# Zeroed products ahead of the input, the first weights in a tile of their own, and one input tile on another queue, in a two-layer DeltaNet and attention kernel

## The chip, the core and the metric

The kernel runs on one core of a Trainium2 chip. The metric is the device time of one execution in microseconds (us), lower is better; the text gives the median of the runs. TensorE (PE in the profile, with its weight loads as PEld) multiplies, VectorE (DVE), ScalarE (ACT) and GpSimd (POOL) do the elementwise work, and SyncE (SP) issues transfers. ScalarE issues transfers too, on a queue of its own. All engines run their own instruction lists and meet only at semaphores.

## The reference

The program computes two layers on an input `x` of 1024 tokens by 1024 channels, in float32. Layer 0 is a gated DeltaNet: one projection, a short causal convolution with SiLU on q, k and v, the delta rule in chunks, a gated RMS norm and an output projection. Layer 1 is sliding-window attention with sinks and rotary positions.

```python
def reference(x, a_w_in, a_conv, a_a_log, ..., ln_g, ln_b):
    for i in range(DEPTH):                      # DEPTH = 2
        if kind == 0:
            y = _gated_deltanet(x, a_w_in[j], a_conv[j], a_a_log[j], a_dt_bias[j], a_norm_g[j], a_w_out[j])
        elif kind == 1:
            y = _swa_sinks(x, b_w_in[j], b_sinks[j], b_w_out[j], pos)
        ...
        x = _layernorm(DEEPNORM_ALPHA * x + y, ln_g[i], ln_b[i])

def _gated_deltanet(x, w_in, conv_w, a_log, dt_bias, norm_g, w_out):
    qkv, z, beta_logit, a_logit = jnp.split(x @ w_in, ...)     # w_in: 1024 x 4112
    qkv = _causal_conv_silu(qkv, conv_w)
    ...                                                        # the delta rule in chunks
    o = _rmsnorm(_unchunk(o), norm_g).reshape(bsz, t_len, GDN_V)
    o = o * jax.nn.silu(z.astype(f32))
    return o.astype(x.dtype) @ w_out
```

## The kernel before, in words

Every projection keeps float32 accuracy by splitting both factors into a high and a low part and adding three products: high by high, high by low, low by high. TensorE wants the channels of `x` on the partitions, and the input comes with tokens there, so the kernel begins by turning it.

**The start.** SP issues eight transfers of 512 KB, one for each tile `t` of 128 tokens, into `tok` (L492), and then four small ones: the convolution's rows (L493), two bias rows and the norm's gains (L494 to L496). ScalarE issues the 16 gate columns of the weight matrix into the front of `w_raw` (`fetch(-1)`, L1151). GpSimd makes the identity, a triangle and zeroed stretches (L594 to L605), each of which counts up `s_const`.

`turn_input(t)` (L715 to L724) waits for tile `t` and turns it in two halves, `n = 2t` and `n = 2t + 1`, each of four 128x128 transposes into one of four PSUM banks. For each half ScalarE rounds the bank to `act_hi` (L1177), then VectorE subtracts to get `act_lo` (L1476), and a bank is free for half `n` once VectorE is done with half `n - 4` (`s_xlo`). TensorE's list is: tiles 0 to 4, then the first half of the gates' product on 512 tokens (`project_input_gates(0, 0)`, L688, which waits for the first eight `act_lo`), tile 5, the second half of that product, tile 6, six products of the first projection tile (`project(0, ...)`, L708), tile 7, the turned convolution rows (L740), and the rest of the projection.

**The weights.** A projection tile `w` is 1024 x 128. ScalarE fetches it into `w_raw` (`fetch(w)`, L1154), rounds it to `w_hi` (`high(w)`, L1160), and VectorE subtracts to get `w_lo` (`low(w)`, L1463). There is one `w_raw`, and the gate columns sit in it too, so `fetch(0)` waits for VectorE's part of the gate columns (L1469) and is issued ahead of half 4 (`FETCH_AT`). `high(0)` stands ahead of half 10 (`HIGH_AT`) on ScalarE, `low(0)` ahead of half 10 on VectorE.

**What follows.** 64 groups of 24 products each (32 weight tiles by two halves of 512 tokens) are laid out for TensorE, ScalarE and VectorE by a table of places (`plan`), with the delta rule of eight heads put between them. For each head VectorE makes `nT`, SP carries its diagonal blocks out and in, GpSimd inverts them in 31 steps (L643, L646), SP carries them back (L527), VectorE sets them out (L1660 to L1663), and TensorE's `level(h, 0)` (L839) waits for that. Layer 0's output stage, layer 1's projections and attention, and its output stage follow.

Only the two buffers `k_dec[1]` and `state` of the later work matter here: `k_dec[1]` is first written for head 1, `state` after the first chunk of head 0.

Of the kernel before, what the change touches and what calls it, by code (L numbers as in the profile page):

```python
# [21 lines left out]
F32 = mybir.dt.float32  # L22
# [4 lines left out]
P = 128  # L27
# [159 lines left out]
def hybrid_trunk(nc, x, a_w_in, a_conv, a_a_log, a_dt_bias, a_norm_g, a_w_out, b_w_in, b_sinks, b_w_out,  # L187
# [9 lines left out]
    with ctx:  # L197
        def sem(name):
            return ctx.enter_context(nc.semaphore(name))
# [154 lines left out]

        s_const = sem("s_const")
        s_x = [sem(f"s_x{t}") for t in range(NT)]
        s_small = sem("s_small")
        s_crow = sem("s_crow")
        s_gates = sem("s_gates")
        s_xtr = sem("s_xtr")  # L360
# [2 lines left out]
        s_ctr = sem("s_ctr")  # L363
        s_cw = sem("s_cw")
        s_wraw = sem("s_wraw")
        s_whi = sem("s_whi")
        s_wlo = sem("s_wlo")
        s_group = sem("s_group")
# [108 lines left out]
        def bank_free(eng, g):  # L477
# [3 lines left out]
            else:  # L481
                eng.wait_ge(s_zt, g - QKV_GROUPS + 1)

        def channel_tile(w):

            return (w % 3) * GH + w // 3 if w < QKV_TILES else w
# [2 lines left out]
        @block.sync  # L489
        def _(sp):  # L490
            for t in range(NT):
                sp.dma_start(tok[:, t, :], x[0, t * P:(t + 1) * P, :]).then_inc(s_x[t], 16)  # L492
            sp.dma_start(conv_rows, a_conv[0].rearrange("k (w p) -> (k w) p", p=P)).then_inc(s_crow, 16)  # L493
            sp.dma_start(bias2[:, 0, :], a_dt_bias[0].partition_broadcast(P)).then_inc(s_small, 16)  # L494
            sp.dma_start(bias2[:, 1, :], a_a_log[0].partition_broadcast(P)).then_inc(s_small, 16)
            sp.dma_start(norm_g[:, :], a_norm_g[0].rearrange("(p a) -> p a", a=1)).then_inc(s_small, 16)  # L496

            sp.wait_ge(s_gr, 2)
            sp.dma_start(gc_rows.rearrange("r (c j) -> (r c) j", c=4), o_tok[0:64, 0, :]).then_inc(s_gio, 16)
# [6 lines left out]
            for h in range(GH):  # L506

                sp.wait_ge(s_m, NT * (h + 1))
                for b in range(4):
                    sp.dma_start(blocks_in[h % 2].rearrange("(c b) j i -> b j c i", b=4)[b],  # L510
                                 nT[h % 2][32 * b:32 * b + 32, :, 32 * b:32 * b + 32]).then_inc(s_pin, 16)
                sp.wait_ge(s_pin, 64 * (h + 1))
                for g in range(4):
                    sp.dma_start(blocks[32 * g:32 * g + 32, :, :], blocks_in[h % 2]).then_inc(s_pb, 16)

                if h + 1 < GH:
                    gc_broadcast(h + 1)
                sp.wait_ge(s_inv, h + 1)
                for g in range(4):
                    sp.dma_start(blocks_out[h % 2][:, g:32:4, :], inverse[32 * g:32 * g + 32, :, :]).then_inc(s_pout, 16)  # L520
                sp.wait_ge(s_pout, 64 * (h + 1))
                if h >= 2:
                    sp.wait_ge(s_y, NT * (h - 1))
                elif h == 0:
                    sp.wait_ge(s_const, 14)
                for b in range(4):
                    sp.dma_start(xT[h % 2][32 * b:32 * b + 32, :, 32 * b:32 * b + 32],  # L527
                                 blocks_out[h % 2].rearrange("(c b) j i -> b j c i", b=4)[b]).then_inc(s_xt, 16)
# [62 lines left out]
        @block.gpsimd  # L591
        def _(pool):
            steps = Link(pool, s_const)
            steps.next(pool.memset(ident[:, :], 0.0))  # L594
            steps.next(pool.memset(tri, 1.0))
            steps.next(pool.memset(w_raw[:, :, 16:P], 0.0))
# [82 lines left out]

        @block.tensor  # L680
        def _(pe):
            pe.wait_ge(s_const, 6)

            def project_input_gates(b, k0):

# [49 lines left out]
            project(0, 0)  # L735
            project(0, STEP)
            turn_input(NT // 2 + 3)
            pe.wait_ge(s_crow, 16)
            rows = CONV_K * QKV_TILES
            pe.transpose(ps[:, 2, 0:rows], conv_rows, ident[0:rows, 0:rows]).then_inc(s_ctr, 1)  # L740
            for q in range(2 * STEP, GROUP, STEP):
# [401 lines left out]
        def _(act):  # L1143
            own = Link(act, s_act)

            def fetch(w):

                if w >= 0:
                    act.wait_ge(s_wlo, w + 1)
                if w < 0:  # L1150
                    act.dma_start(w_raw[:, :, 0:16], wa_tiles[:, :, GATE_COL:GDN_IN]).then_inc(s_wraw, 16)  # L1151
                else:
                    c0 = P * channel_tile(w)
                    act.dma_start(w_raw[:, :, :], wa_tiles[:, :, c0:c0 + P]).then_inc(s_wraw, 16)  # L1154

            def high(w):
                act.wait_ge(s_wraw, 16 * (w + 2))
                if w >= 1:
                    act.wait_ge(*((s_gates, 2) if w == 1 else (s_group, 2 * w - 2)))
                act.activation(w_hi[w % 2][:, :, :], w_raw[:, :, :], ACT.Copy).then_inc(s_whi, 1)  # L1160

            fetch(-1)
            act.wait_ge(s_const, 4)
            act.activation(w_hi[1][:, :, 32:P], w_raw[:, :, 32:P], ACT.Copy)
            for n in range(2 * NT):
                if n == 2:
                    act.wait_ge(s_wraw, 16)
                    act.activation(w_hi[1][:, :, 0:16], w_raw[:, :, 0:16], ACT.Copy).then_inc(s_whi, 1)
                if n == FETCH_AT:
                    fetch(0)  # L1170
                if n == HIGH_AT:
                    high(0)
# [285 lines left out]
        def _(dve):  # L1458
            own = Link(dve, s_dve)

            def low(w):
                dve.wait_ge(s_whi, w + 2)
                dve.tensor_tensor(w_lo[w % 2][:, :, :], w_raw[:, :, :], w_hi[w % 2][:, :, :].bitcast(F32),  # L1463
                                  ALU.subtract).then_inc(s_wlo, 1)

            for n in range(2 * NT):
# [4 lines left out]
                if n == HIGH_AT:  # L1471
# [7 lines left out]
            dve.wait_ge(s_ctr, 1)  # L1479
            dve.tensor_scalar(convw[:, :, :], ps[:, 2, 0:CONV_K * QKV_TILES].rearrange("p (k w) -> p k w", k=CONV_K),  # L1480
                              0.5, None, ALU.mult).then_inc(s_cw, 1)
            dve.wait_ge(s_small, 48)
            own.next(dve.tensor_scalar(norm_g[:, :], norm_g[:, :], 0.5, None, ALU.mult))
            def piece(g, k):

# [449 lines left out]
```

## Time and profile before

| | |
|---|---|
| median of 3 runs | 1054.86 us |
| lowest and highest | 1054.53 and 1057.03 us |
| the profiled execution: its own time | 1057.3 us |
| the profiled execution: its span | 1055.6 us |
| TensorE busy | 1027.4 us, 97% of the span |
| VectorE, ScalarE, GpSimd busy | 679.0, 498.6, 250.0 us |
| TensorE's granted clock, mean | 0.99 of full speed |

Times in the trace count from the first recorded instruction. A row of a timeline is a run of like instructions: start, how long they took together, the engine, the line, and in brackets how long the engine was idle before them and what released it. The releaser is inferred: a wait on several semaphores is put down to the one that came last by the profile, and where the engine named had long been done, it was another. The page's own row for the clock is in tenths of full speed.

### The profile page before, as it was taken

The page shows a single profiled execution, that of the slowest core. Times are in us where ns is not written, and L with a number is a line of the kernel's source. Part 1 is how long each engine was busy: PE and PEld are TensorE (multiplying, and loading weights), DVE is VectorE, ACT ScalarE, POOL GpSimd, SP SyncE. Part 2 cuts the span into 40 slices and gives each one's busy share as a digit, 9 for nine tenths or more (in the row PEclk, how much of TensorE's full clock was granted, in tenths as well). Part 3 has the DMA queues.
Part 4 walks back from the last instruction along what each step waited for, and adds up shares of the span by engine and source line. Part 5 has one row for each costly group of instructions (what it writes and reads, how often), then busy time and mean ns, then how long its engine had stood idle before and what let it go on. Part 6 is the DMA issues. An engine that isn't in the chain of part 4 may idle for free. (4 is left out here: it accounts for less than half of the span.)

```text
span 1055.6 us, 17698 instructions
## 1 busy us (share of the span) xinstructions
PE 1027.4 (97%) x6286; PEld 841.8 (80%) x6286; DVE 679.0 (64%) x1591; ACT 498.6 (47%) x1389; POOL 250.0 (24%) x585
## 2 busy tenths in 40 slices
PE   7999799999999999999999999999999999999997
PEld 6888688888888887888888888888877777777885
DVE  4676657676767675744457767535367877789655
ACT  5555457575756665644354112202155566568000
POOL 1008482827373746462000000000100000000000
PEclk9999899999999999999999999999999999999999
DMA  6222303122221212213114212202001000013211
GB/s 204 62 84 50 88 21 71 46 55 62 47 70 37 80 36 61 55 43 109 40 41 160 80 60 61 71 1 70 20 1 38 24 21 21 21 61 100 100 41 60
DMA packets 84215, 62.64 MB, mean 59 GB/s; under 512 B 32128, under 2 KB 74272, under 8 KB 84128
## 3 DMA queue, kind: packets, MB, share of 16 engines
q1 hardware_dynamic: 49808, 44.68, 14.1%
q10 hardware_dynamic: 34320, 16.84, 6.1%
q8 instruction: 50, 0.82, 0.3%
q14 instruction: 37, 0.30, 0.1%
HBM read 55.18 MB, written 6.32 MB: 58 GB/s over the span
## 5 line engine op out<-in xcount | busy, mean ns | idle before, releaser
L708 PE MATMUL ps<-act_hi,w_hi 128*128 128x512 f32 x512 | 225.7, 441 | 0.2 <-DVE w_lo L1463 0.2
L708 PE MATMUL ps<-act_hi,w_lo 128*128 128x512 f32 x512 | 202.6, 396 | 0.0
L708 PE MATMUL ps<-act_lo,w_hi 128*128 128x512 f32 x512 | 201.5, 394 | 0.0
L1512 DVE SCALAR_TENSOR_TENSOR tok<-xs,convw,tok 128x512 f32<-128x512 f32 x144 | 115.6, 803 | 21.4 <-ACT xs L1208 19.5
L643 POOL TENSOR_TENSOR rank<-inverse,tok 128x60 f32<-128x60 f32 (+24 forms) x248 | 97.8, 394 | 97.1 <-DMA tok<-blocks_in 78.8
L708 PEld LDWEIGHTS ps<-act_hi,w_lo 128*128 128x128 f32 x512 | 97.0, 189 | 21.7
L708 PEld LDWEIGHTS ps<-act_hi,w_hi 128*128 128x128 f32 x512 | 97.7, 191 | 12.1 <-issue 0.4
L708 PEld LDWEIGHTS ps<-act_lo,w_hi 128*128 128x128 f32 x512 | 98.1, 192 | 10.0
L646 POOL TENSOR_TENSOR inverse<-inverse,rank 128x60 f32<-128x60 f32 (+24 forms) x248 | 95.8, 386 | 19.4
L906 PE MATMUL ps<-wo_hi,act_hi 128*128 128x512 f32 x224 | 88.4, 395 | 1.0 <-DVE wo_lo L1615 1.0
L906 PE MATMUL ps<-wo_lo,act_hi 128*128 128x512 f32 x224 | 87.6, 391 | 0.0
L906 PE MATMUL ps<-wo_hi,act_lo 128*128 128x512 f32 x210 | 81.9, 390 | 0.0
L1363 ACT ACTIVATE mv<-mv 128x1 f32<-128x1 f32 x16 | 3.3, 204 | 125.7 <-DVE mv L1759 125.7
L1074 PE MATMUL ps<-act_hi,z_hi 128*128 128x512 f32 x128 | 52.2, 407 | 0.8 <-DVE zg L1873 0.8
L1074 PE MATMUL ps<-act_hi,z_lo 128*128 128x512 f32 x128 | 51.9, 405 | 0.0
L1074 PE MATMUL ps<-act_lo,z_hi 128*128 128x512 f32 x128 | 51.8, 405 | 0.0
L978 PE MATMUL ps<-ws_hi,act_hi 128*128 128x512 f32 x128 | 51.6, 403 | 0.0
L906 PEld LDWEIGHTS ps<-wo_hi,act_hi 128*128 128x128 f32 x224 | 42.1, 188 | 11.7 <-issue 2.6
L978 PE MATMUL ps<-ws_hi,act_lo 128*128 128x512 f32 x128 | 50.3, 393 | 0.0
L978 PE MATMUL ps<-ws_lo,act_hi 128*128 128x512 f32 x128 | 49.9, 389 | 0.0
L906 PEld LDWEIGHTS ps<-wo_lo,act_hi 128*128 128x128 f32 x224 | 42.1, 188 | 8.8 <-DVE act_lo L1604 0.2
L1405 ACT ACTIVATE logit_far<-logit_far,sm_neg 128x256 f32<-128x256 f32 x64 | 31.7, 499 | 34.0 <-DVE sm_off L1841 34.0
(273 smaller groups left out, 2252.8 us busy)
## 6 DMA issues: line engine op xcount, KB each, us to landing
w_raw<-in_a_w_in ACTq DMA_DIRECT2D x32, 512.0 KB, 4.2
tok<-in_x SPq DMA_DIRECT2D x8, 512.0 KB, 6.9
decay<-gc_rows SPq DMA_DIRECT2D x8, 512.0 KB, 4.8
tok<-blocks_in SPq DMA_DIRECT2D x32, 128.0 KB, 2.6
xres<-in_x SPq DMA_DIRECT2D x8, 512.0 KB, 3.6
ws_raw<-in_b_w_in SPq DMA_DIRECT2D x16, 256.0 KB, 2.7
z_raw<-in_b_w_in SPq DMA_DIRECT2D x8, 512.0 KB, 3.9
out<-yr SPq DMA_DIRECT2D x7, 512.0 KB, 2.6
```

Of the source, the lines that this page charges most:

```text
L643: inner.next(pool.tensor_tensor(part, inverse[:, 0:rows, m:m + 1].broadcast_to([P, rows, w]), blocks[:, m:m + 1, m + 1:32].broadcast_to([P ...
L646: last = pool.tensor_tensor(inverse[:, 0:rows, m + 1:32], inverse[:, 0:rows, m + 1:32], part, ALU.add)
L708: mm = pe.matmul(ps[:, g % 2, :], lhs[:, k, :], rhs[:, k, HALF * b:HALF * (b + 1)], start=(i == 0), stop=(i == GROUP - 1))
L906: mm = pe.matmul(ps[:, OUT_BANKS[t] + half, :], lhs[:, k, t * P:(t + 1) * P], rhs[:, HALF * half:HALF * (half + 1)], start=(k == 0 and j = ...
L978: mm = pe.matmul(ps[:, TOKEN_BANKS[n % 4], 0:w], lhs[:, k, t * P:(t + 1) * P], rhs, start=(k == 0 and j == 0), stop=(k == NK - 1 and j == ...
L1074: mm = pe.matmul(ps[:, GATE_BANK, :], lhs[:, k, :], rhs[:, k, HALF * b:HALF * (b + 1)], start=(i == 0), stop=(i == GROUP - 1))
L1363: act.activation(mv[:, t % 2, 3:4], mv[:, t % 2, 2:3], ACT.Sqrt).then_inc(s["sqrt"], 1)
L1405: act.activation(logit[u % 4][:, i, :], logit[u % 4][:, i, :], ACT.Exp, bias=sm["neg"][:, u % 2, i:i + 1], accum_out=sm["sum"][:, u % 2, i ...
L1512: ins = dve.scalar_tensor_tensor(conv[b], xs[:, b, k:k + HALF], convw[:, k, tile:tile + 1], conv[b], ALU.mult, ALU.add)
```

## The change

**TensorE.** Its list now begins with a wait for `s_const` 1 and nine products of `state` with itself, 128x128 float32, into PSUM bank 2, whose result nobody reads. GpSimd zeroes `state` for this ahead of all else and waits until that is done; every later count of `s_const` is one higher.

TensorE before, from its first instruction to the turn of tile 1 (`ps<-ident,tok` is a transpose of the input, `s_x0` the arrival of tile 0):

```order
L680 UNCONDITIONAL_BRANCH [waits barrier_Pool_Activation_PE_DVE_SP_release]
L722 MATMUL ps<-ident,tok 128x128 [waits s_x0,s_const]
L722 MATMUL ps<-ident,tok 128x128 x7
L722 MATMUL ps<-ident,tok 128x128 [waits s_x1]
L722 MATMUL ps<-ident,tok 128x128 x7
```

And the changed one, the same place:

```order
L687 UNCONDITIONAL_BRANCH [waits barrier_Pool_Activation_PE_DVE_SP_release]
L691 MATMUL ps<-state 128x128 [waits s_const]
L691 MATMUL ps<-state 128x128 x8
L732 MATMUL ps<-ident,tok 128x128 [waits s_x0,s_const]
L732 MATMUL ps<-ident,tok 128x128 x7
L732 MATMUL ps<-ident,tok 128x128 [waits s_x1]
L732 MATMUL ps<-ident,tok 128x128 x7
```

Nine instructions stand ahead of the first transpose; behind them the order is as it was.

**ScalarE.** Tile 1 of the input is issued from here, first of all, and no longer by SP. The weights of tile 0 go to `k_dec[1]` (`raw(0)`) instead of `w_raw`, with a semaphore of their own (`s_wfirst`), so `fetch(0)` waits for nothing any more, and it stands ahead of half 1 instead of half 4. ScalarE's list before, up to `high(0)` and the next fetch:

```order
L1151 DMA w_raw<-in_a_w_in 128x8x16
L1164 ACT_TABLE_LOAD
L1164 ACTIVATE w_hi<-w_raw 128x8x96 [waits s_const]
L1177 ACTIVATE act_hi<-ps 128x4x128 [waits s_xtr] x2
L1168 ACTIVATE w_hi<-w_raw 128x8x16 [waits s_wraw]
L1177 ACTIVATE act_hi<-ps 128x4x128 [waits s_xtr] x2
L1154 DMA w_raw<-in_a_w_in 128x8x128 [waits s_wlo]
L1177 ACTIVATE act_hi<-ps 128x4x128 [waits s_xtr] x6
L1160 ACTIVATE w_hi<-w_raw 128x1024 [waits s_wraw]
L1177 ACTIVATE act_hi<-ps 128x4x128 [waits s_xtr] x3
L1154 DMA w_raw<-in_a_w_in 128x8x128 [waits s_wlo]
```

And the changed one:

```order
L1175 DMA tok<-in_x 128x1024
L1161 DMA w_raw<-in_a_w_in 128x8x16
L1178 ACT_TABLE_LOAD
L1178 ACTIVATE w_hi<-w_raw 128x8x96 [waits s_const]
L1191 ACTIVATE act_hi<-ps 128x4x128 [waits s_xtr]
L1164 DMA k_dec<-in_a_w_in 128x8x128
L1191 ACTIVATE act_hi<-ps 128x4x128 [waits s_xtr]
L1182 ACTIVATE w_hi<-w_raw 128x8x16 [waits s_wraw]
L1191 ACTIVATE act_hi<-ps 128x4x128 [waits s_xtr] x8
L1173 ACTIVATE w_hi<-k_dec 128x1024 [waits s_wfirst]
L1191 ACTIVATE act_hi<-ps 128x4x128 [waits s_xtr] x3
L1164 DMA w_raw<-in_a_w_in 128x8x128 [waits s_wlo]
```

The fetch of the first weights has moved three halves forward and lost its wait; `high(0)` and the fetch of tile 1 stand where they stood.

**SP.** It issues seven input tiles and the four small transfers. These four share one semaphore, `s_crow`, so TensorE's turn of the convolution rows (L740 before) and VectorE's work on the gains (L1483 before) now wait for all four.

The whole diff:

```diff
--- before.py
+++ after.py
@@ -354,7 +354,6 @@
 
         s_const = sem("s_const")
         s_x = [sem(f"s_x{t}") for t in range(NT)]
-        s_small = sem("s_small")
         s_crow = sem("s_crow")
         s_gates = sem("s_gates")
         s_xtr = sem("s_xtr")
@@ -363,6 +362,7 @@
         s_ctr = sem("s_ctr")
         s_cw = sem("s_cw")
         s_wraw = sem("s_wraw")
+        s_wfirst = sem("s_wfirst")
         s_whi = sem("s_whi")
         s_wlo = sem("s_wlo")
         s_group = sem("s_group")
@@ -481,6 +481,10 @@
             else:
                 eng.wait_ge(s_zt, g - QKV_GROUPS + 1)
 
+        def raw(w):
+
+            return w_raw[:, :, :] if w else k_dec[1][:, :, :]
+
         def channel_tile(w):
 
             return (w % 3) * GH + w // 3 if w < QKV_TILES else w
@@ -489,11 +493,12 @@
         @block.sync
         def _(sp):
             for t in range(NT):
-                sp.dma_start(tok[:, t, :], x[0, t * P:(t + 1) * P, :]).then_inc(s_x[t], 16)
+                if t != 1:
+                    sp.dma_start(tok[:, t, :], x[0, t * P:(t + 1) * P, :]).then_inc(s_x[t], 16)
             sp.dma_start(conv_rows, a_conv[0].rearrange("k (w p) -> (k w) p", p=P)).then_inc(s_crow, 16)
-            sp.dma_start(bias2[:, 0, :], a_dt_bias[0].partition_broadcast(P)).then_inc(s_small, 16)
-            sp.dma_start(bias2[:, 1, :], a_a_log[0].partition_broadcast(P)).then_inc(s_small, 16)
-            sp.dma_start(norm_g[:, :], a_norm_g[0].rearrange("(p a) -> p a", a=1)).then_inc(s_small, 16)
+            sp.dma_start(bias2[:, 0, :], a_dt_bias[0].partition_broadcast(P)).then_inc(s_crow, 16)
+            sp.dma_start(bias2[:, 1, :], a_a_log[0].partition_broadcast(P)).then_inc(s_crow, 16)
+            sp.dma_start(norm_g[:, :], a_norm_g[0].rearrange("(p a) -> p a", a=1)).then_inc(s_crow, 16)
 
             sp.wait_ge(s_gr, 2)
             sp.dma_start(gc_rows.rearrange("r (c j) -> (r c) j", c=4), o_tok[0:64, 0, :]).then_inc(s_gio, 16)
@@ -522,7 +527,7 @@
                 if h >= 2:
                     sp.wait_ge(s_y, NT * (h - 1))
                 elif h == 0:
-                    sp.wait_ge(s_const, 14)
+                    sp.wait_ge(s_const, 15)
                 for b in range(4):
                     sp.dma_start(xT[h % 2][32 * b:32 * b + 32, :, 32 * b:32 * b + 32],
                                  blocks_out[h % 2].rearrange("(c b) j i -> b j c i", b=4)[b]).then_inc(s_xt, 16)
@@ -591,6 +596,8 @@
         @block.gpsimd
         def _(pool):
             steps = Link(pool, s_const)
+            steps.next(pool.memset(state[:, :], 0.0))
+            steps.wait()
             steps.next(pool.memset(ident[:, :], 0.0))
             steps.next(pool.memset(tri, 1.0))
             steps.next(pool.memset(w_raw[:, :, 16:P], 0.0))
@@ -679,7 +686,10 @@
 
         @block.tensor
         def _(pe):
-            pe.wait_ge(s_const, 6)
+            pe.wait_ge(s_const, 1)
+            for i in range(9):
+                pe.matmul(ps[:, 2, 0:P], state[:, :], state[:, :], start=True, stop=True)
+            pe.wait_ge(s_const, 7)
 
             def project_input_gates(b, k0):
 
@@ -735,7 +745,7 @@
             project(0, 0)
             project(0, STEP)
             turn_input(NT // 2 + 3)
-            pe.wait_ge(s_crow, 16)
+            pe.wait_ge(s_crow, 64)
             rows = CONV_K * QKV_TILES
             pe.transpose(ps[:, 2, 0:rows], conv_rows, ident[0:rows, 0:rows]).then_inc(s_ctr, 1)
             for q in range(2 * STEP, GROUP, STEP):
@@ -1145,28 +1155,32 @@
 
             def fetch(w):
 
-                if w >= 0:
+                if w >= 1:
                     act.wait_ge(s_wlo, w + 1)
                 if w < 0:
                     act.dma_start(w_raw[:, :, 0:16], wa_tiles[:, :, GATE_COL:GDN_IN]).then_inc(s_wraw, 16)
                 else:
                     c0 = P * channel_tile(w)
-                    act.dma_start(w_raw[:, :, :], wa_tiles[:, :, c0:c0 + P]).then_inc(s_wraw, 16)
+                    act.dma_start(raw(w), wa_tiles[:, :, c0:c0 + P]).then_inc((s_wraw, s_wfirst)[w == 0], 16)
 
             def high(w):
-                act.wait_ge(s_wraw, 16 * (w + 2))
+                if w:
+                    act.wait_ge(s_wraw, 16 * (w + 1))
+                else:
+                    act.wait_ge(s_wfirst, 16)
                 if w >= 1:
                     act.wait_ge(*((s_gates, 2) if w == 1 else (s_group, 2 * w - 2)))
-                act.activation(w_hi[w % 2][:, :, :], w_raw[:, :, :], ACT.Copy).then_inc(s_whi, 1)
-
+                act.activation(w_hi[w % 2][:, :, :], raw(w), ACT.Copy).then_inc(s_whi, 1)
+
+            act.dma_start(tok[:, 1, :], x[0, P:2 * P, :]).then_inc(s_x[1], 16)
             fetch(-1)
-            act.wait_ge(s_const, 4)
+            act.wait_ge(s_const, 5)
             act.activation(w_hi[1][:, :, 32:P], w_raw[:, :, 32:P], ACT.Copy)
             for n in range(2 * NT):
                 if n == 2:
                     act.wait_ge(s_wraw, 16)
                     act.activation(w_hi[1][:, :, 0:16], w_raw[:, :, 0:16], ACT.Copy).then_inc(s_whi, 1)
-                if n == FETCH_AT:
+                if n == 1:
                     fetch(0)
                 if n == HIGH_AT:
                     high(0)
@@ -1460,7 +1474,7 @@
 
             def low(w):
                 dve.wait_ge(s_whi, w + 2)
-                dve.tensor_tensor(w_lo[w % 2][:, :, :], w_raw[:, :, :], w_hi[w % 2][:, :, :].bitcast(F32),
+                dve.tensor_tensor(w_lo[w % 2][:, :, :], raw(w), w_hi[w % 2][:, :, :].bitcast(F32),
                                   ALU.subtract).then_inc(s_wlo, 1)
 
             for n in range(2 * NT):
@@ -1479,7 +1493,7 @@
             dve.wait_ge(s_ctr, 1)
             dve.tensor_scalar(convw[:, :, :], ps[:, 2, 0:CONV_K * QKV_TILES].rearrange("p (k w) -> p k w", k=CONV_K),
                               0.5, None, ALU.mult).then_inc(s_cw, 1)
-            dve.wait_ge(s_small, 48)
+            dve.wait_ge(s_crow, 64)
             own.next(dve.tensor_scalar(norm_g[:, :], norm_g[:, :], 0.5, None, ALU.mult))
             def piece(g, k):
 
```

## Rows read from the trace of the kernel before

**Rows 1.** The page: busy time of TensorE, share of the span, instructions.

```profile
PE 1027.4 (97%) x6286; PEld 841.8 (80%) x6286; DVE 679.0 (64%) x1591; ACT 498.6 (47%) x1389; POOL 250.0 (24%) x585
```

**Rows 2.** Waits of TensorE, longest in total: us, times, longest.

```profile
PE ps L839 <- DVE tok L1663: 5.5, 2, 5.3
```

**Rows 3.** Timeline of TensorE, the start: start us, us, instruction, idle before.

```profile
4.63 7.47 PE L722 MATMUL ps<-ident,tok 128*128 128x128 f32 x40 [4.63 <-POOL xT L605]
...
12.75 0.47 PE L688 MATMUL ps<-act_hi,w_hi 128*128 128x512 f32 x1 [0.65 <-DVE act_lo L1476]
...
18.59 0.47 PE L708 MATMUL ps<-act_hi,w_hi 128*128 128x512 f32 x1 [0.17 <-DVE w_lo L1463]
...
20.93 0.25 PE L740 MATMUL ps<-ident,qT 96*128 96x96 f32 x1
```

**Rows 4.** Windows, TensorE: us, busy (instructions), granted clock, DMA share, GB/s.

```profile
9.00:10.00 1.00, 1.00 (x6) 1.00 1.02 406
10.00:11.00 1.00, 1.00 (x10) 1.00 1.06 422
```

**Rows 5.** Timeline of VectorE, the start.

```profile
6.39 0.69 DVE L1476 TENSOR_TENSOR act_lo<-ps,act_hi 128x512 fp32r<-128x512 f32 x1 [6.39 <-ACT act_hi L1177]
...
10.70 3.10 DVE L1476 TENSOR_TENSOR act_lo<-ps,act_hi 128x512 fp32r<-128x512 f32 x5 [0.16 <-ACT act_hi L1177]
17.22 1.23 DVE L1463 TENSOR_TENSOR w_lo<-w_raw,w_hi 128x1024 fp32r<-128x1024 f32 x1 [3.42 <-ACT w_hi L1160]
```

**Rows 6.** Timeline of ScalarE, the start.

```profile
5.76 0.60 ACT L1177 ACTIVATE act_hi<-ps 128x512 fp32r<-128x512 f32 x1 [2.32 <-PE ps L722]
...
8.37 0.37 ACTq L1154 DMA_DIRECT2D w_raw<-in_a_w_in  x1
...
16.12 1.06 ACT L1160 ACTIVATE w_hi<-w_raw 128x1024 fp32r<-128x1024 f32 x1 [3.38 <-DMA w_raw<-in_a_w_in]
```

**Rows 7.** Issues at 0.80, 2.19, 2.93, 0.81, 8.37 and 18.48 us, to landing.

```profile
tok<-in_x SPq DMA_DIRECT2D x1, 512.0 KB, 3.7
...
tok<-in_x SPq DMA_DIRECT2D x1, 512.0 KB, 6.7
...
tok<-in_x SPq DMA_DIRECT2D x1, 512.0 KB, 7.2
...
w_raw<-in_a_w_in ACTq DMA_DIRECT2D x1, 64.0 KB, 4.2
...
w_raw<-in_a_w_in ACTq DMA_DIRECT2D x1, 512.0 KB, 7.7
...
w_raw<-in_a_w_in ACTq DMA_DIRECT2D x1, 512.0 KB, 4.2
```

**Rows 8.** DMA queues from 12 to 13 us (q1 SP's, q10 ScalarE's): packets, MB.

```profile
q1 hardware_dynamic: 85, 0.34, 84.3%
q10 hardware_dynamic: 86, 0.04, 15.5%
```

**Rows 9.** Timeline of TensorE: float32 products of 128x128, one behind the other.

```profile
63.53 0.38 PE L812 MATMUL ps<-kT 128*128 128x128 f32 x2
63.75 0.39 PE L814 MATMUL ps<-qT,kT 128*128 128x128 f32 x2
```

**Rows 10.** Timeline of GpSimd: its first fill.

```profile
0.80 0.20 POOL L594 MEMSET ident<- 128x128 f32 x1 [0.29 <-POOLq L1924]
```

**Rows 11.** Windows, all engines: PE, PEld, DVE, ACT, POOL busy, clock, DMA.

```profile
120.00:140.00 20.00, 15.48 (x146) 12.02 (x147) 7.46 (x16) 5.96 (x23) 8.91 (x25) 0.66 0.34 84
124.00:126.00 2.00, 1.49 (x33) 1.42 (x34) 1.26 (x4) 0.70 (x2) 0.00 (x0) 0.50 0.63 188
400.00:410.00 10.00, 8.97 (x61) 7.59 (x61) 5.29 (x10) 3.64 (x9) 7.06 (x20) 0.83 0.26 68
```

**Rows 12.** The last small transfer, issued at 6.31 us, to landing.

```profile
norm_g<-in_a_norm_g SPq DMA_DIRECT2D x1, 0.5 KB, 9.4
```

## The prediction

> **What bounds the kernel now.** I read four views in turn: the page, the waits of TensorE, the timelines of the start, the transfers. TensorE is busy 97% of the span [rows 1], so time is lost where it idles or runs slowly, and a microsecond that its list starts earlier is one at the end, unless a later wait swallows it. Its largest wait, 5.3 us at L839, is for head 0's inverse [rows 2]. That chain (VectorE's `nT`, transfers, GpSimd's 31 steps, transfers) begins with results of TensorE's earlier groups, so it moves along with TensorE and swallows nothing. The change touches the first 20 us only.
>
> There the reader should see this. TensorE starts at 4.63, when tile 0 has landed (0.80 + 3.7 = 4.5) [rows 3, 7]. GpSimd, which the row names as releaser, was only filling buffers that nobody waits for. TensorE turns the input without pause until 12.1, idles 0.65 until 12.75 for VectorE's eighth `act_lo`, and idles 0.17 at 18.59 for the low part of the first weights. After that it is fed until L839. So only two dates count: 12.75, the start of the gates' product (call it G), and 18.59, the start of the first projection (call it W).
>
> **The start is slow for two reasons.** First, TensorE ran at its lower level (1.2 GHz): 6 transposes began from 9 to 10 us and 10 from 10 to 11 [rows 4]. The clock column says 1.00 in both, so before about 10.3 I trust the count and not the column. A half tile of four transposes thus took 0.85 (0.213 each). Second, the input arrives at 406 to 422 GB/s with the DMA engines fully busy [rows 4]: tile 3 at 2.19 + 6.7 = 8.9, tile 4 at 2.93 + 7.2 = 10.1, so one per 1.2 us, two halves [rows 7]. VectorE at full pace needs 3.10/5 = 0.62 per half [rows 5], the same as the transfers' 0.6. Raising the clock can win back only what TensorE lost against those two.
>
> **Part 1, the nine products.** GpSimd's first fill runs from 0.80 to 1.00 [rows 10]; it is now that of `state`, so the products start at about 1.1. A float32 product of this size shows as two records and takes 0.22 at full speed (63.53 to 63.75) [rows 9], so 0.44 at the lower level; nine are 9 x 0.44 = 4.0 us, and end at 5.1. If the clock rises on the way they end earlier. No row shows products of zeros at the start. The bounds for the end are 1.1 + 9 x 0.22 = 3.1 (full speed throughout, which costs nothing, since tile 0 is not there) and 5.1. I take 5.1 as the nearer, since the first 5.6 us of work before ran at the lower level. That is 0.5 later than 4.63. GpSimd's other fills come 0.25 later; the last that matters was due before 3, hidden behind tile 0.
>
> **Part 2, tile 1 on ScalarE's queue.** It was behind tile 0 on one queue and now runs beside it. From 12 to 13 us, when both queues had data, they moved 85 and 86 packets, of 4 KB and 0.5 KB [rows 8]: packet for packet. Tiles 0 and 1 have equal packets, so tile 0 gets half the engines until it is done. Bounds: it lands as before at 4.5 if the queue of tile 1 starts late, or one tile's time (1.2) later, at 5.7. I take 5.2, the middle, since the gate columns, which went beside tile 0 before (landed 0.81 + 4.2 = 5.0 [rows 7]), now stand behind tile 1. So TensorE's first transpose is at about 5.3 instead of 4.63, and the nine products hardly cost anything beyond that. The gate columns land near 6.5; ScalarE wants them at about 7.3, and if they come at 8 everything behind half 1 is 0.7 later.
>
> The Trainium skill ("DMA: Bandwidth & Descriptors", Queues, rings and completion order) says that each engine goes round its queues packet by packet; the trace agrees (85 to 86). By that rule alone tile 0 would land at the late end, 5.7, and G would lose 0.5 of the gain below.
>
> **G.** Before, VectorE began its first half at 6.39, 1.76 behind the first transpose (0.85 of transposes, the rest pipeline and ScalarE's 0.60) [rows 5, 6]. At full clock four transposes are 0.43, so the lag is 1.34, and VectorE starts at 5.3 + 1.34 = 6.65. From the start of half 0 to the end of half 7 it needs 7 x 0.61 + 0.3 for the gate columns + 0.69 = 5.3, and 0.15 passes to TensorE: G = 12.1. That is 0.65 earlier than 12.75. If the clock is still low for the first two halves, the lag is as before and G = 12.5; if tile 0 is back at 4.5, G = 11.4. So G gains 0.2 to 1.35.
>
> The skill's page "TensorE: Matmul & The Clock Gate" (Part 4: PE-mode transpose) says that transposes do not bring the full clock. The trace disagrees: the count rises from 6 to 10 per microsecond within the transposes [rows 4], with nothing else on TensorE. By the page the transposes would still run slowly behind the nine products, and the sum would be G unchanged and no gain, 1054.9; that is inside the second rival, and the row leaves it a chance of 3 in 100.
>
> **W, part 3, the first weights.** Before, they were issued at 8.37 and landed at 16.1 (7.7 us), where the next ones, on an empty machine, took 4.2 [rows 7]; ScalarE idled 3.38 for them, rounded them at 16.12, VectorE subtracted at 17.22, TensorE went at 18.59 [rows 3, 5, 6]. So TensorE follows the landing by 2.5. Now they are issued near 6.3, behind ScalarE's first half. But the engines were saturated from 2.5 to 15, so issuing earlier doesn't make all the data arrive earlier; it only changes who is last. Packet for packet, the 1024 packets of 0.5 KB get ahead at the speed of the large ones: with three tiles left (384 packets) they are 384 on when the tiles are done, and 640 remain. At the bound of no gain they still land at 16.1; at the bound of full priority they land 4.2 + about 3 after the issue, at 13.5. I take 15.5: they pass only the four small transfers and profit from the fuller first microsecond. W gains 0.6, and the first weights stay the last thing to arrive.
>
> The gain is the smaller of G's (0.65, plus the 0.17 of idle) and W's (0.6): **0.6 us**. What is late next is the weights again.
>
> **Small edits at nothing.** The joint semaphore: the last of the four landed at 6.31 + 9.4 = 15.7 [rows 12], TensorE turns the convolution rows at 20.93 [rows 3], 5 us of cover; without it the price is the overlap. The issue of tile 1 takes ScalarE 0.4 before anything else, covered by 5 us of waiting; the issue of the weights (0.37) stands before half 1, covered while the transposes of that half run, otherwise 0.2. `k_dec[1]` is idle until head 1.
>
> **The sum.** The profiled execution took 1057.3 for a span of 1055.6; minus 0.6 that is 1056.7. It is 2.4 above the median of 1054.86, and the runs spread by 2.5. The same saving from the median gives **1054.3 us**.
>
> **The rivals.**
> - *The start gains more (17%).* The weights pass two tiles and land by 15, tile 0 keeps its date. Then G decides: 1.35 + 0.17, or 1.5, 1053.4. For: the gate columns passed quickly before. Against: rows 8, which give small packets one turn per large one.
> - *The start gets slower (13%).* The clock isn't high during the transposes, for zeros don't raise it or transposes don't hold it, and tile 0 lands at 5.7. TensorE then starts 1.2 late at 5.85 at the lower level, VectorE at 7.6, and four halves at 0.85 pass before the rise at 10.3: G = 13.5, 0.75 late, 1055.6. It decides once G passes 12.9. Against: the transposes alone raised the clock before [rows 4].
> - *The clock later falls less (12%).* From 120 to 140 us the mean clock is 0.66 [rows 11], so 0.34 x 20 / 0.5 = 13.6 us at the lower level, following the 5.3 of idle at L839. TensorE resumed at 124.5 (1.49 busy to 126), so some 12 of these were work, which lost 6 us. From 400 to 410 (0.83) another 3.4, or 1.7 us. If the shifted list misses the fall, the gain is 0.6 + 6 to 7.7, some 1048. For: 0.65 of idle at 12.75 brought no fall, so idleness alone doesn't decide. Against: four executions lie within 2.8 us, so it looks regular.
> - *It falls more (8%).* The same mechanism the other way: two more slow stretches of 3.4 us near TensorE's smaller pauses cost 2 x 1.7, minus 0.6, 1057.7, and one more stretch makes it 1059. It decides from the second stretch.
> - *Forecast (50%).*
>
> **How the numbers follow.** About 0.3% (3.2 us) is what a measurement of this kernel can tell from no change. No case of the start reaches it; only the clock does. Faster 0.14 (the third rival and a little of the first with a shorter slow stretch), slower 0.08, same 0.78. The range is that of the starts, 1053.2 to 1055.6, widened by the 1.7 of one slow stretch either way, less what the same run could cancel: 1051.8 to 1056.8; the other two clock cases, 0.20 together, are left out.
>
> **What would show it.** Nine pairs of records from 1.1 to about 5; the first transpose between 4.6 and 5.7; transposes at 10 per microsecond from the start or soon after; the gates' product at 12.1; the weights landing near 15.5, ScalarE still idle before rounding them, the first projection at 18.0; L839's wait unchanged at 5.3. Wrong if the weights land before 14, if the first transpose is later than 5.8, or if the clock from 120 to 140 isn't near 0.66.

## The result: 1065.3 us against 1055.5, slower

The changed kernel took 1065.32 us (median of 4 runs, 1064.21 to 1065.72), the kernel before 1055.45 beside it (1054.53 to 1057.03): ratio 1.0087, 95% interval 1.0075 to 1.0099. The profiled execution took 1065.32 for a span of 1063.6, against 1057.3 and 1055.6. The forecast was 1054.3, 1051.8 to 1056.8.

The page of the changed kernel, whose first line answers to [rows 1]:

```profile
PE 1031.4 (97%) x6304; PEld 845.6 (80%) x6304; DVE 679.3 (64%) x1591; ACT 498.1 (47%) x1389; POOL 250.3 (24%) x586
```

TensorE is 4.0 us busier, about what the nine products take. The other 4 us are idleness, which the timeline of TensorE at the start shows (it answers to [rows 3]):

```profile
1.06 4.03 PE L691 MATMUL ps<-state 128*128 128x128 f32 x18 [1.06 <-POOL state L599]
5.88 1.94 PE L732 MATMUL ps<-ident,tok 128*128 128x128 f32 x16 [0.79 <-DMA tok<-in_x]
8.01 1.16 PE L732 MATMUL ps<-ident,tok 128*128 128x128 f32 x8 [0.19 <-DVE act_lo L1490]
16.86 3.65 PE L732 MATMUL ps<-ident,tok 128*128 128x128 f32 x16 [7.69 <-DVE act_lo L1490]
20.31 0.77 PE L698 MATMUL ps<-act_hi,w_hi 128*128 128x512 f32 x1
...
26.46 0.47 PE L718 MATMUL ps<-act_hi,w_hi 128*128 128x512 f32 x1
```

Behind tile 2 TensorE stands for 7.69 us. The first projection begins at 26.46 instead of 18.59, 7.87 late, and the end is 8.0 late: the whole loss in the trace stands in the first 27 us. The medians lie 9.9 apart and not 8.0, mostly because the traced execution of the kernel before was one of its long ones: over all chips, its executions from 1056.5 us up had a mean granted clock of 0.990, as the traced one, and those with 0.993 took 1054.2 to 1055.6.

Who is late is two steps back. In ScalarE's timeline of the kernel before, the round of the gate columns waits for nothing:

```profile
7.11 0.30 ACT L1168 ACTIVATE w_hi<-w_raw 128x128 fp32r<-128x128 f32 x1
```

In the changed kernel it is L1182:

```profile
7.04 0.60 ACT L1191 ACTIVATE act_hi<-ps 128x512 fp32r<-128x512 f32 x1
15.20 0.31 ACT L1182 ACTIVATE w_hi<-w_raw 128x128 fp32r<-128x128 f32 x1 [7.57 <-DMA w_raw<-in_a_w_in]
15.42 2.04 ACT L1191 ACTIVATE act_hi<-ps 128x512 fp32r<-128x512 f32 x4
```

ScalarE has the halves of tile 1 in front of it and doesn't touch them: its next instruction wants the gate columns. VectorE waits for ScalarE, TensorE for a bank from VectorE. The transfers of the changed kernel from issue to landing, tile 0 (issued at 0.81), the gate columns (1.25) and the first projection weights (6.55), answer to [rows 7]:

```profile
tok<-in_x SPq DMA_DIRECT2D x1, 512.0 KB, 4.9
...
w_raw<-in_a_w_in ACTq DMA_DIRECT2D x1, 64.0 KB, 13.9
...
k_dec<-in_a_w_in ACTq DMA_DIRECT2D x1, 512.0 KB, 10.1
```

The smallest of them, 64 KB, took 13.9 us where it had taken 4.2. The queues tell why. The kernel before, 3.5 to 4.5 us, when the gate columns were moved (packets, MB, share of 16 engines):

```profile
q10 hardware_dynamic: 1027, 0.06, 70.4%
q1 hardware_dynamic: 72, 0.23, 56.6%
```

The changed kernel, 6 to 7 us:

```profile
q1 hardware_dynamic: 112, 0.39, 97.5%
q10 hardware_dynamic: 111, 0.01, 7.6%
```

The gate columns are rows of 64 bytes, 1024 packets. Before, they passed in one microsecond, beside 72 packets of SP's queue. Now each waits for its turn behind a packet of 4 KB, 111 to 112, as [rows 8] had it for other transfers: 1024/111 = 9.2 us from about 5.4 on. (The Trainium skill, "DMA: Bandwidth & Descriptors", Queues, rings and completion order, has this rule; the 111 to 112 agree with it. The 1027 to 72 of the kernel before are no even turns, and the experiments take that up.)

The clock suffers from the wait too. Windows of the changed kernel, with TensorE busy, then its loads, VectorE, ScalarE, GpSimd, then the clock:

```profile
10.00:12.00 2.00, 0.00 (x0) 0.00 (x0) 0.00 (x0) 0.00 (x0) 0.00 (x0) 0.90 1.05 402
12.00:20.00 8.00, 3.13 (x15) 3.17 (x16) 4.00 (x7) 3.75 (x8) 0.00 (x0) 0.50 0.50 136
...
128.00:148.00 20.00, 15.92 (x146) 12.44 (x147) 7.62 (x16) 5.96 (x23) 10.36 (x29) 0.66 0.30 79
```

It falls to the lower level in the wait, so the 16 transposes behind it took 3.65. The last row answers to [rows 11]: 8 us later in the list, the same 0.66, so the later fall of the clock neither helped nor hurt.

### The profile page after: what moved, and what is told of

Its sections match the earlier page's. It is cut to its first block and busy times, and to the rows that moved or that the text cites. A ratio compares the mean times of both kernels' runs of the same rounds, so it can differ in the third digit from the quotient of the medians.

```text
span 1063.6 us, 17735 instructions
## 1 busy us (share of the span) xinstructions
PE 1031.4 (97%) x6304; PEld 845.6 (80%) x6304; DVE 679.3 (64%) x1591; ACT 498.1 (47%) x1389; POOL 250.3 (24%) x586
## 3 DMA queue, kind: packets, MB, share of 16 engines
q1 hardware_dynamic: 49664, 44.15, 13.9%
```

## The experiments

Times are medians; each ratio is to the kernel before on the same chip.

**Which part.** First the changed kernel with two of ScalarE's issues swapped:

```diff
-            act.dma_start(tok[:, 1, :], x[0, P:2 * P, :]).then_inc(s_x[1], 16)
             fetch(-1)
+            act.dma_start(tok[:, 1, :], x[0, P:2 * P, :]).then_inc(s_x[1], 16)
```

> The changed kernel with two transfers swapped on ScalarE's queue: the gate columns first, then input tile 1. Theory of turns (the engines give each queue one packet in turn, so the 1024 packets of 64 B that stood behind tile 1 moved no faster than SP's 4 KB packets): the gate columns land before 6 us, TensorE's 7.7 us wait and the fall of the clock at 11.6 go, and the time is 1053.5 to 1055.5, that of the kernel before less some tenths. Rival (the two queues together, or the earlier weights, hold the input back whatever the order): the gate columns are early, yet the time stays above 1059.

Measured: 1058.46 us, ratio 1.0020 (1.0012 to 1.0029). The gate columns land after 4.4, the 7.7 us wait is gone, 7 us come back. What remains is another wait, since tile 1 now shares with the tiles behind it and lands at 1.31 + 7.1 = 8.4. The clock falls in that wait too (granted 0.50 from 10 to 12 us), so the 32 transposes behind it run slowly, and the first projection begins at 19.86, 1.3 later than before. TensorE's timeline:

```profile
5.05 1.46 PE L732 MATMUL ps<-ident,tok 128*128 128x128 f32 x8
8.43 5.38 PE L732 MATMUL ps<-ident,tok 128*128 128x128 f32 x32 [1.92 <-DMA tok<-in_x]
```

The expected 1053.5 to 1055.5 was too low, and this wait is what it left out.

Then the kernel before with tile 1 issued by ScalarE ahead of `fetch(-1)`, and nothing else:

```diff
-                sp.dma_start(tok[:, t, :], ...).then_inc(s_x[t], 16)
+                if t != 1:
+                    sp.dma_start(tok[:, t, :], ...).then_inc(s_x[t], 16)
...
+            act.dma_start(tok[:, 1, :], x[0, P:2 * P, :]).then_inc(s_x[1], 16)
             fetch(-1)
```

> The kernel before with one part of the change alone: input tile 1 issued by ScalarE ahead of the gate columns. Theory of turns: the gate columns land near 15 us instead of 5.0, TensorE idles 7 to 8 us between tiles 2 and 3, and the time is 1063 to 1066. Rival (the nine products or the early weights in their own tile make the stall): no stall, 1054 to 1057.

Measured: 1064.62, ratio 1.0077 (1.0062 to 1.0091); the gate columns took 13.4 from their issue at 1.25. This one part makes the loss. The idle is 5.28 and not 7 to 8, mostly because the transposes before it ran longer, at the lower level (24 in 5.30 us), and in part because the gate columns landed 0.5 earlier than in the changed kernel. The opposite, the changed kernel with tile 1 back in SP's loop and the ScalarE issue gone:

```diff
-                if t != 1:
-                    sp.dma_start(tok[:, t, :], ...).then_inc(s_x[t], 16)
+                sp.dma_start(tok[:, t, :], ...).then_inc(s_x[t], 16)
...
-            act.dma_start(tok[:, 1, :], x[0, P:2 * P, :]).then_inc(s_x[1], 16)
             fetch(-1)
```

> The changed kernel with tile 1 issued by SP again, so with the nine products, the first weights in their own tile and the joint semaphore. Theory of turns: gate columns at 5 us, no stall, 1053 to 1055. Rival (as above): above 1059. If the start is limited by the weights' landing, it gains 0.3 to 0.8 us on the kernel before; if by VectorE, 1.0 to 1.5.

Measured: 1056.51, ratio 1.0001 (0.9992 to 1.0009): no loss, and not the expected gain either. Its timeline of TensorE shows why no gain:

```profile
12.03 0.47 PE L697 MATMUL ps<-act_hi,w_hi 128*128 128x512 f32 x1 [0.63 <-DVE act_lo L1488]
...
18.69 0.47 PE L717 MATMUL ps<-act_hi,w_hi 128*128 128x512 f32 x1 [0.98 <-DVE w_lo L1475]
```

The gates' product is 0.72 earlier than before, and the first projection isn't: the weights land at 6.16 + 10.0 = 16.2, against 16.1 before, though issued 2.2 us earlier.

**Why the gate columns used to be fast.** If the engines give turns by packets, half the packet size should halve the wait:

```diff
-                    sp.dma_start(tok[:, t, :], ...).then_inc(s_x[t], 16)
+                    for c in range(2):
+                        sp.dma_start(tok[:, t, HALF * c:HALF * (c + 1)],
+                                     x[0, t * P:(t + 1) * P, HALF * c:HALF * (c + 1)]).then_inc(s_x[t], 16)
...
-                pe.wait_ge(s_x[t], 16)
+                pe.wait_ge(s_x[t], 16 if t == 1 else 32)
```

> The changed kernel with each of SP's input tiles in two transfers of 2 KB rows instead of one of 4 KB rows, so the same bytes in twice as many packets. Theory of turns: each packet of the gate columns waits for half as many bytes; 64 packets per engine need 64 turns of about 0.09 us, 6 us from about 5.3, so they land at 11 to 12 us instead of 15.2, the stall is about 4 us, and the time 1059 to 1062. Rival (the gate columns wait for the bytes queued before them): they land at 15 or later and the time is 1064 to 1066.

Measured: 1056.60, ratio 1.0008 (0.9999 to 1.0018). Both theories fell: the gate columns landed at 1.25 + 6.1 = 7.4, not at 11 to 12. From 5 to 6 us:

```profile
q1 hardware_dynamic: 127, 0.23, 66.8%
q10 hardware_dynamic: 830, 0.05, 57.1%
```

830 to 127 is no even turn. In this kernel, as in the one before, the gate columns pass just as SP's queue ends what was issued ahead of them: the second half of tile 0 here, tile 0 there. For the kernel before, a closer look, from 3.8 to 4.2 us; by 3.7 SP's queue had moved 128 packets, as many as one tile has:

```profile
q10 hardware_dynamic: 730, 0.05, 125.2%
q1 hardware_dynamic: 17, 0.03, 21.1%
```

SP's queue moves little in these 0.4 us; from 5 to 6 us it moves 114 packets again. The new theory: transfers become ready in the order of issue over both queues, and where the gate columns are ready before SP's next tile, they meet a queue that is nearly dry. In the changed kernel SP's tile 2 was issued beside them, and its queue had no such gap. No view shows when packets become ready, so this stays an inference, which the next two runs test. If it holds, no tile need be moved at all; it is enough to issue the gate columns a little later in the kernel before:

```diff
-            fetch(-1)
             act.wait_ge(s_const, 4)
+            fetch(-1)
```

> The kernel before, all tiles on SP's queue; the only edit lets ScalarE issue the gate columns after its wait for GpSimd's fills, near 2.0 us instead of 0.81, so behind SP's issues of tiles 1 and 2. Half packets (4 KB to 2 KB) had brought the gate columns to about 7.4 us, where pure turns gave 11 to 12, so turns alone fall short. Theory of order: the packets of all transfers become ready in the order of issue, and small packets run fast only while the other queue is dry; in the kernel before this was between tiles 0 and 1. With two tiles ahead of them the gate columns find SP's queue full, get one turn per 4 KB packet, land after 12 us, and the time is 1061 to 1066. Rival (what counts is only that tile 1 stands ahead of them on ScalarE's own queue): they land 1.2 us later than before, at 6 to 7, and the time stays at 1055 to 1057.

Measured: 1063.90, ratio 1.0074 (1.0057 to 1.0091). Issued at 2.0 instead of 0.81, they take 12.5; nothing stands ahead of them on their own queue. TensorE's timeline and the queues from 7 to 8 us:

```profile
4.58 5.35 PE L722 MATMUL ps<-ident,tok 128*128 128x128 f32 x24 [4.58 <-POOL xT L605]
16.19 3.65 PE L722 MATMUL ps<-ident,tok 128*128 128x128 f32 x16 [6.26 <-DVE act_lo L1476]
```

```profile
q1 hardware_dynamic: 89, 0.35, 90.6%
q10 hardware_dynamic: 110, 0.01, 7.4%
```

SP's queue was not full for all of it. From 6 to 7 us, when it had moved three tiles (those issued ahead of the gate columns), some of them passed quickly again:

```profile
q1 hardware_dynamic: 88, 0.29, 74.0%
q10 hardware_dynamic: 384, 0.02, 26.2%
```

That is the gap where the theory of order puts it, but only about a third of the gate columns used it, and the rest took turns to the end. 1.2 us at the issue cost 8.3 in time. Next the converse, the changed kernel with SP's tile 2 held back behind the issue of the gate columns:

```diff
+                if t == 2:
+                    sp.wait_ge(s_const, 4)
                 if t != 1:
```

> The changed kernel, where SP holds tile 2 back until GpSimd's fills are at the fourth, near 2.2 us instead of 1.25, so that the gate columns (1.25) are issued before it. Theory of order: SP's queue runs dry after tile 0, the gate columns pass there and land at 6 to 7.5 us, the 7.7 us wait goes, and the time is 1055.5 to 1058. Rival (standing behind tile 1 on ScalarE's queue is what delays them): they land at 15 as in the changed kernel, 1064 to 1066.

Measured: 1058.10, ratio 1.0025 (1.0011 to 1.0040), the runs from 1055.90 to 1061.88. The gate columns take 8.3 instead of 13.9, and the wait of 7.7 shrinks to 0.5. The direction is as the theory of order says; the size isn't, since they were expected at 6 to 7.5 and landed at 9.5. Most of them passed early (ScalarE's queue moved 935 packets from 5 to 6 us, SP's 31), a rest did not, and why a rest stays behind is open. So the order of issue decides whether the gate columns find a gap; what makes the gap, and how much of them fits in, is not shown.

**What the other two parts are worth.** The kernel before with the zeroed `state` and the nine products alone:

```diff
+            steps.next(pool.memset(state[:, :], 0.0))
+            steps.wait()
...
+            pe.wait_ge(s_const, 1)
+            for i in range(9):
+                pe.matmul(ps[:, 2, 0:P], state[:, :], state[:, :], start=True, stop=True)
```

> The kernel before with the nine products of zeros alone. If the clock rises early, the gates' product begins at 12.0 to 12.2 instead of 12.75, but the first weights, issued earlier too, land near 16 as before and the first projection stays at 18.5 to 18.7: 1055 to 1056.5, the kernel before within 0.5 us. Rival (the clock's gain is kept): 0.7 us faster. If products of zeros don't raise the clock: 12.9 to 13.3, and 0.2 to 0.5 us slower.

Measured: 1056.26, ratio 1.0006 (0.9995 to 1.0017), no difference. The products do raise the clock. TensorE from 6 to 7 us, in the kernel before and here:

```profile
6.00:7.00 1.00, 1.00 (x6) 1.00 1.06 422
...
6.00:7.00 1.00, 1.00 (x11) 1.00 1.04 414
```

Nothing but the end of the products holds the transposes back, which begin at 5.06 instead of 4.63, and the gates' product is at 11.95, 0.8 earlier. Then

```profile
18.52 0.47 PE L713 MATMUL ps<-act_hi,w_hi 128*128 128x512 f32 x1 [0.92 <-DVE w_lo L1468]
```

the first weights take it back, landing at 8.24 + 7.8 = 16.0. The date that bounds is the weights'. So in the next run (weights_between: the changed kernel, edited) SP issues them among the tiles, all tiles stay on SP's queue, and ScalarE issues neither:

```diff
             for t in range(NT):
+                if t == 5:
+                    sp.dma_start(raw(0), wa_tiles[:, :, 0:P]).then_inc(s_wfirst, 16)
...
-            act.dma_start(tok[:, 1, :], x[0, P:2 * P, :]).then_inc(s_x[1], 16)
             fetch(-1)
...
-                if n == 1:
-                    fetch(0)
```

> The nine products, all input tiles on SP's queue, and the first projection weights issued by SP between tiles 4 and 5. If the first weights are what holds the start once the clock is up, they land near 12.5 us instead of 16.2, ScalarE's wait for them goes, the first projection begins at 17.6 to 17.9 instead of 18.6 to 18.7, and the time is 0.8 to 1.1 us below that with tile 1 back on SP's queue, about 1055. Rival (tiles 5 to 7, each 1.8 us later, become the wait): the first projection stays at 18.5 or later and so does the time.

Measured: 1054.98, ratio 0.9995 (0.9985 to 1.0005). They land at 3.36 + 8.6 = 12.0, nothing waits for them, and

```profile
17.45 0.48 PE L719 MATMUL ps<-act_hi,w_hi 128*128 128x512 f32 x1
```

is 1.14 earlier than before, 0.15 more than expected. The time isn't resolved from no change. The trace of this run leads by 1.13 at L850 (5.08 of idle from 118.10, before from 119.23), and ended 0.1 behind: part of the lead went in a pause of 0.60 ahead of 729.40, in layer 1, which the kernel before doesn't have:

```profile
729.40 0.66 PE L1044 MATMUL ps<-ident,qr 128*128 128x128 f32 x4 [0.60 <-DVE qr L1827]
```

The same without the products, and once more with them, on one chip:

```diff
-            for i in range(9):
-                pe.matmul(ps[:, 2, 0:P], state[:, :], state[:, :], start=True, stop=True)
```

> As weights_between (first projection weights issued by SP between tiles 4 and 5), without the nine products. If the start is bounded by the later of the two dates, the clock's and the weights', the gates' product is back at 12.75 and the first projection at 18.3 to 18.5: 0.9 to 1.1 us slower than weights_between, equal to the kernel before. Rival (the weights alone bring the gain): the first projection at 17.5 and the time of weights_between.

> weights_between once more, beside the version without the products on the same chip: 0.9 to 1.1 us faster than that, and 0.5 to 1.0 us faster than the kernel before. If its earlier start is taken back by later waits, no difference beyond 0.3 us.

Measured: without 1055.73, ratio 1.0002 (0.9993 to 1.0012); with them 1054.72, 0.9995 (0.9985 to 1.0005). The 1.0 between the medians is of the expected size, but each interval takes in the other's ratio. In the profiled executions the first projection began at 17.73 without the products and at 17.00 with them, and the same kernel with them had given 17.45, so one trace leaves 0.3 to 0.7 for the products, and not 0.9 to 1.1. Of the 1.14 gained at the first projection, 0.86 came without them. A part of that was luck: here the clock rose by itself near 8.5 and not 10.3, and the gates' product began at 12.29 and not 12.75. TensorE in windows without the products:

```profile
7.00:8.00 1.00, 1.00 (x7) 1.00 0.99 397
8.00:9.00 1.00, 1.00 (x8) 1.00 1.00 401
9.00:10.00 1.00, 1.00 (x10) 1.00 1.07 354
```

**The share of the clock in the loss.** The changed kernel with TensorE kept busy through the wait:

```diff
             for t in range(NT // 2 + 1):
+                if t == 3:
+                    for i in range(34):
+                        pe.matmul(ps[:, 2, 0:P], state[:, :], state[:, :], start=True, stop=True)
                 turn_input(t)
```

> The changed kernel with 34 more products of zeros between the turns of tiles 2 and 3, 34 x 0.22 = 7.5 us, so that TensorE is busy while it waits for the gate columns. If the fall of the clock in that wait costs the changed kernel anything, the clock no longer falls at 11.6, the 16 transposes behind the wait take 2.1 us instead of 3.65, the first projection begins 1.5 to 2.5 us earlier than 26.5, and the time is 1063 to 1064 instead of 1065.3. Rival (VectorE's pace behind the gate columns sets the date whatever the clock): the first projection moves by less than 0.5 us and the time stays above 1064.8.

Measured: 1061.87, ratio 1.0062 (1.0047 to 1.0078). The 16 transposes behind the wait:

```profile
16.65 2.36 PE L732 MATMUL ps<-ident,tok 128*128 128x128 f32 x16
...
25.08 0.47 PE L718 MATMUL ps<-act_hi,w_hi 128*128 128x512 f32 x1
```

2.36 instead of 3.65, and the first projection 1.4 earlier than 26.46, a little less than expected. So of 7.9 us the clock made 1.4 at most and the late gate columns the rest. The median fell by 3.4, more than expected, and the traces, which end 2.8 apart, say where most of it is. The 1.4 of the start are one half. The other came later: around 140 us this trace gained another 2.2 on that of the changed kernel, with a mean granted clock of 0.83 from 120 to 150 us against 0.77, and around 190 it gave 1.1 back, with 0.91 from 180 to 200 against 1.00.

**The later fall of the clock differs from trace to trace.** TensorE from 120 to 150 us in the kernel before, and in the changed kernel with the gate columns first:

```profile
120.00:150.00 30.00, 25.48 (x202) 0.77 0.28 70
...
120.00:150.00 30.00, 24.86 (x212) 0.89 0.29 79
```

Compared with the kernel before, the second was 1.1 late ahead of the low stretch and 1.3 early behind it: 2.4 us that the start didn't make, and the reason why this trace ended 0.1 before that of the kernel before, while its median is 2.5 above. The trace without the products in the last pair ended 2.8 before it, and 1.4 of that came near 405 us, where its mean granted clock from 395 to 420 was 1.00 against 0.93. So here the start of a trace is compared by the date of the first projection, and its end can't tell two kernels apart that are within 2 to 3 us; only medians of many executions can. Whether the change of the start has an influence on the later fall isn't shown: the traces of the kernel before and of the changed kernel have the same 0.77.

## Why the prediction was wrong, step by step

- **The step that failed is in part 2**: "The gate columns land near 6.5; ScalarE wants them at about 7.3, and if they come at 8 everything behind half 1 is 0.7 later." They landed at 15.2. The prediction has no working for 6.5. The rule was there one step earlier, 85 packets to 86 [rows 8]; it was applied to tiles 0 and 1, to the first weights, and even as the argument against its first rival, but not to the transfer with the smallest packets, now behind tile 1. By it, 1024 packets beside a full queue are the 9.2 us worked out above. That the same transfer had landed after 4.2 [rows 7] is no price of the transfer: it depended on the place in the order of issue, as the run with a late issue of the gate columns shows without moving a tile.
- **The bound that was set wrong**: 8 us as the late end had no row behind it. With 15.2 the prediction's own working gives 15.2 - 7.3 = 7.9 later, 1054.3 + 7.9 = 1062.2, and with its 1.7 for the clock 1064.
- Tile 0: 4.9 after its issue, 5.7, the late end of the bounds. First transpose at 5.88, not 5.3, past the 5.8 that the prediction itself had set as a sign of being wrong.
- The nine products: 4.0 us from 1.06 to 5.09, as forecast. They raise the clock and the transposes keep it (16 in 1.94 us), as [rows 4] said; the sentence of the Trainium skill ("TensorE: Matmul & The Clock Gate", Part 4: PE-mode transpose) that transposes don't bring the full clock is contradicted again, most plainly by the run without the products, where they alone brought it by 9 us (10 of them from 9 to 10 us).
- The gates' product at 12.1: with tile 1 back on SP's queue it was 12.03, with the products alone 11.95. With tile 1 on ScalarE's queue and no long stall (the run with half packets) it was 12.52, near the prediction's own figure for tile 0 at its late end (0.5 later than 12.1). So the products gave what was forecast, and part 2 took most of it back even where the gate columns came in time.
- The weights: in the changed kernel they landed at 6.55 + 10.1 = 16.7 and nothing waited for them: ScalarE, held up by the gate columns, came to round them only at 21.04. With tile 1 back on SP's queue "the first weights stay the last thing to arrive" was right, but the 0.6 of gain was 0: they landed at 16.2 instead of 15.5, at the bound of no gain (16.1).
- The stall at L839 is 5.0 instead of 5.3, and the clock's later fall the same 0.66: the third and fourth rivals played no part in this trace. In traces of other runs the later fall was shorter, and the gain was about 2.4 us, not the 6 to 7.7 of the third rival.
- The low end of the starts in the range, 1053.2, has no term behind it: the first rival's own sum gives 1053.4. It decides nothing.
- The second rival named slower, but by 0.75 and by another mechanism.

## What to carry to other kernels

A transfer of many small packets is priced by packets and not by bytes: beside a full queue it gets a turn per large packet, so 64 KB took 13.9 us here where 512 KB took 4.9. Issue it first, and before the other queue gets its second transfer; its earlier speed proves nothing once anything is issued ahead of it. Before raising an engine's clock or moving a fetch, look which transfer lands last: behind all tiles, an issue 2.2 us earlier didn't bring the weights earlier, while a place between tiles 4 and 5 on SP's queue brought them 4 us earlier.

## What the runs showed of the hardware that was not expected

- A delay of 1.2 us in one issue (0.81 to 2.0) made a 64 KB transfer take 12.5 us instead of 4.2.
- Two queues don't always share evenly by packets: 111 to 112 was seen in the middle of SP's stream, but 1027 to 72, 830 to 127 and 384 to 88 where SP's queue came to the end of the transfers that were issued ahead of the gate columns. That its next packets weren't ready is the likely reason; no view shows it.
- The clock of the start rises at different times though TensorE's work before it is the same: the count of transposes rose near 10.3 us in one kernel and near 8.5 in another, both beginning them at 4.6 to 4.7.
- The spread of the kernel before (1053.35 to 1058.24 in 77 executions on three chips) goes with its mean granted clock: 0.995 for the shortest three, 0.990 for all above 1056.5.
